# Small latent projections of branch D placed between the big projection blocks, in a two-layer trunk kernel

## What is computed

```
h = _rms(x, p['norm1_g']) * (1 + sc1) + sh1
aq, ak, av, bq, bk, bv, cq, ck, cv, dqa, dckv, dkr, gates = _split_in(h @ p['w_in'])
aq = pos(_rms(aq.reshape(B, T, A_HEADS, 2, A_QK), p['a_qk_g'][0]))
...
dq = (_rms(dqa, p['d_qnorm_g']) @ p['w_d_qb']).reshape(B, T, D_HEADS, D_QK)
dq = _rms(dq, p['d_qk_g'][0])
dckv = _rms(dckv, p['d_kvnorm_g'])
kd, vd = _mla_kv(dckv, dkr, p['w_d_kvb'], p['d_qk_g'][1])
```

## Time and profile before

| | us |
|---|---|
| median of 3 runs | 5418.61 (5416.52 to 5420.11) |
| profiled execution | 5413.07 |
| its span | 5411.3 |
| PE busy | 5099.5 (94%) |
| DVE busy | 3206.5 (59%) |
| ACT, POOL busy | 1676.5, 1325.4 |
| this stage, layer 0 and layer 1 | 241.1 and 234.6 |

### The profile page before, as it was taken

The page is one execution under the profiler, slowest core; times in us unless marked ns, Lnnn a source line. Parts: engine busy times, 40 slices in busy tenths (PEclk is TensorE's granted clock), DMA queues, the critical chain, the costliest instruction groups (busy, mean ns, idle before and its releaser), DMA issues.

```text
span 5411.3 us, 68396 instructions
## 1 busy us (share of the span) xinstructions
PE 5099.5 (94%) x25512; PEld 4124.9 (76%) x25512; DVE 3206.5 (59%) x7229; ACT 1676.5 (31%) x2610; POOL 1325.4 (24%) x858
## 2 busy tenths in 40 slices
PE   4979999889999999999989799998899999999999
PEld 1846688677888887888868467877788888788887
DVE  1556411107998995666654763111488998766666
ACT  2325422222333332222232353212233333322222
POOL 1310022214344331111123001213244344211111
PEclk6978999999999999999999799999999999999999
DMA  6200021264877878888831001222367877888886
GB/s 228 71 29 1 11 73 65 74 242 170 270 239 260 281 258 308 289 288 291 293 121 58 15 1 35 68 65 66 131 219 263 280 261 239 316 286 294 291 288 222
DMA packets 349128, 981.98 MB, mean 181 GB/s; under 512 B 31648, under 2 KB 100128, under 8 KB 345504
## 3 DMA queue, kind: packets, MB, share of 16 engines
q1 hardware_dynamic: 215232, 553.19, 31.6%
q0 software_dynamic: 74880, 276.86, 14.6%
q10 hardware_dynamic: 58720, 148.04, 7.0%
HBM read 829.43 MB, written 148.54 MB: 181 GB/s over the span
## 4 chain that ended last, share of the span: by engine, by line
PE 84%; DVE 6%; DMA 3%; ACT 3%; POOL 1%; issue 1%; DVEq 1%; ACTq 0%; POOLq 0%; SPq 0%
PE PS L813 26%; PE PS L773 23%; PE PS L474 15%; PE PS L463 5%; PE PS L795 4%; PE PS L601 3%; PE PS L627 2%; PE PS L464 1%; DVE AR L1183 1%; PE PS L611 1%; POOL HR L1516 1%; PE PS L571 1%; DMA WR<-in_ada 1%; PE PS L761 1%; DVE SM L1222 1%
## 5 line engine op out<-in xcount | busy, mean ns | idle before, releaser
L813 PE MATMUL PS<-HB,VR 128*128 128x512 f32 x6144 | 1397.1, 390 | 17.2 <-DVE HB L1473 17.2
L813 PEld LDWEIGHTS PS<-HB,VR 128*128 128x128 f32 x6144 | 1156.3, 188 | 258.0 <-issue 18.0
L773 PE MATMUL PS<-HR,UR 128*128 128x512 f32 x4128 | 1013.0, 399 | 0.0
L1516 POOL TENSOR_TENSOR UR<-WR,UR 128x1024 fp32r<-128x1024 f32 x212 | 530.6, 2504 | 1838.7 <-ACT UR L995 938.0
L474 PE MATMUL PS<-HR,UR 128*128 128x320 f32 (+1 forms) x5952 | 924.0, 315 | 44.0 <-POOL HR L1516 38.8
L474 PEld LDWEIGHTS PS<-HR,UR 128*128 128x128 f32 x5952 | 888.4, 190 | 69.9 <-issue 47.6
L773 PEld LDWEIGHTS PS<-HR,UR 128*128 128x128 f32 x4128 | 768.2, 190 | 166.9
L1460 DVE TENSOR_TENSOR VR<-HT,VR 128x1024 fp32r<-128x1024 f32 x256 | 313.8, 1226 | 459.7 <-ACT VR L1113 374.4
L1113 ACT CAST VR<-HT 128x1024 fp32r<-128x1024 f32 x256 | 268.8, 1050 | 962.7 <-PE PS L813 960.2
L773 PE MATMUL PS<-HR 128*128 128x512 f32 x2016 | 486.7, 394 | 0.0
L773 PEld LDWEIGHTS PS<-HR 128*128 128x128 f32 x2016 | 372.1, 188 | 73.6
(11 more groups left out here) (183 smaller groups left out, 5975.4 us busy)
## 6 DMA issues: line engine op xcount, KB each, us to landing
WR<-in_uT SPq DMA_DIRECT2D x256, 512.0 KB
HT<-in_vtab SPq DMA_DIRECT2D x256, 512.0 KB, 4.0
activations<-AR ACTq DMA_DIRECT2D x256, 256.0 KB
gates_by_expert<-AR ACTq DMA_DIRECT2D x128, 512.0 KB, 3.5
HW<-activations SPq DMA_DIRECT2D x256, 256.0 KB
WR<-gates_by_expert SPq DMA_DIRECT2D x64, 1024.0 KB
WR<-in_wgate SPq DMA_DIRECT2D x64, 640.0 KB, 3.9
WR<-in_ada SPq DMA_DIRECT2D x24, 1024.0 KB, 4.9
```

What stands on the lines that cost most here:

```text
L773: last = pe.matmul(bank(n % 2), u_part(n, w)[:, c, :], HR[:, h, c, 0:LAT], start=c == 0 and i == 0, stop=c == DC - 1 and i == 2)
L813: last = pe.matmul(bank(d), VR[:, m % 4, w, P * d:P * d + P], HB[:, (m + 1) % 3, h, :], start=m == 0 and i == 0, stop=m == E1 - 1 and i == 2)
L1516: nc.gpsimd.tensor_tensor(dst, src, high.bitcast(F32), ALU.subtract).then_inc(sem_, 1)
```

## The change

The items get a new order: qa, qa, ckv, kr, aq, aq, ak, and from there a small item after each big block: dq0, ak, dk0, bq, dq1, bq, dk1, bk, dq2, cq, dk2, cq, dq3, ck, dk3. `d_values` comes behind them, and `values` comes last, in another order of token tiles, with the last two rotations between its first three blocks. The small items' weights leave the ring: those of dq and of the values of D are loaded at once into the tail columns of all four slots (which only gate blocks used), those of dk into a free part of HT. STD moves from VD to VT, since VT is now written last. The semaphores are counted anew.

```diff
-    items = ([("aq", 0), ("aq", 1), ("ak", 0), ("ak", 1), ("bq", 0), ("bq", 1), ("bk", 0), ("cq", 0), ("cq", 1),
-              ("ck", 0), ("qa", 0), ("qa", 1), ("ckv", 0), ("kr", 0)]
-             + [("dq", h) for h in range(HEADS)] + [("dk", h) for h in range(HEADS)])
+    items = [("qa", 0), ("qa", 1), ("ckv", 0), ("kr", 0), ("aq", 0), ("aq", 1), ("ak", 0), ("dq", 0), ("ak", 1), ("dk", 0),
+             ("bq", 0), ("dq", 1), ("bq", 1), ("dk", 1), ("bk", 0), ("dq", 2), ("cq", 0), ("dk", 2), ("cq", 1), ("dq", 3),
+             ("ck", 0), ("dk", 3)]
...
-        STD = VD.rearrange("p a b -> p (a b)").rearrange("p (a b) -> p a b", a=2)
+        STD = VT[:, 0:3, :].rearrange("p a b -> p (a b)").rearrange("p (a b) -> p a b", a=2)
...
+                sp.dma_start(WR[:, :, D:SLOT], wdq[l]).then_inc(d_in, 16)
                 sp.wait_ge(hr_ready, l * (2 * DC) + DC)
...
+                sp.dma_start(WDK.rearrange("p h d -> p (h d)"), wkv[l]).then_inc(d_in, 16)
...
-                load(l, B_DQ, WR[:, B_DQ % RING, 0:2 * HEADS * D_QK], wdq[l])
-                load(l, B_KV, WR[:, B_KV % RING, 0:HEADS * (D_QK + HD)], wkv[l])
...
+            VALUE_TILES = (3, 2, 4, 1, 0)
+
+            def values(l, n):
+                if n == 0:
+                    pe.wait_ge(y_ready, (l + 1) * NI)
+                pe.wait_ge(split, l * N_SPLIT + (SPLIT_NO[B_V + n] + 1))
+                w = UR[:, SPLIT_NO[B_V + n] % 2]
+                for t in VALUE_TILES:
+                    if n == 0 and t == 4:
+                        pe.wait_ge(dv_out, l + 1)
...
-                for s in range(NI + 2):
-                    if s == N_FM:
-                        values(l)
+                for s in range(NI + 1):
                     if s < NI:
                         if items[s] == ("dk", 0):
                             pe.wait_ge(l_in, l * 96 + 80)
                             pe.wait_ge(yn_ready, l * NN + (norm_no[at_item["ckv", 0]] + 1))
                         project(l, s)
-                    if 1 <= s <= NI:
+                    else:
+                        d_values(l)
+                    if s >= 1:
                         head_sums(l, s - 1)
-                    if s >= 2:
+                    if 2 <= s < NI:
                         rotate(l, s - 2)
-                d_values(l)
+                values(l, 0)
+                rotate(l, NI - 2)
+                values(l, 1)
+                rotate(l, NI - 1)
+                for n in range(2, N_V):
+                    values(l, n)
                 phase_end(pe, l, 1)
...
-                for s in range(NI + 1):
-                    if s < N_FM:
-                        high(l, B_FM + s + 2)
-                    if s == N_FM:
-                        for n in range(2, N_V):
-                            high(l, B_V + n)
-                        used(l, B_V + N_V - 1)
-                        for t in range(TILES):
-                            nc.scalar.copy(VT[:, t if t < 4 else 5, :], bank(t if t < 4 else 7)).then_inc(v_out, 1)
-                    if s < NI:
-                        raw(l, s)
+                for s in range(NI):
+                    if s in block_of:
+                        high(l, B_FM + block_of[s] + 2)
+                    raw(l, s)
                     if s >= 1:
                         std(l, s - 1)
-                used(l, B_KV)
+                act.wait_ge(dv_ready, l + 1)
+                nc.scalar.copy(VD[:, 0:4, :].rearrange("p a b -> p (a b)"), PF[:, 0:1024])
+                nc.scalar.copy(VD[:, 4:6, :].rearrange("p a b -> p (a b)"), bank(7)).then_inc(dv_out, 1)
+                std(l, NI - 1)
+                for n in range(2, N_V):
+                    high(l, B_V + n)
+                used(l, B_V + N_V - 1)
                 act.wait_ge(yn_ready, (l + 1) * NN)
-                nc.scalar.copy(VD.rearrange("p a b -> p (a b)"), PF[:, 0:256 * KTILES])
+                for t in range(TILES):
+                    nc.scalar.copy(VT[:, t if t < 4 else 5, :], bank(t if t < 4 else 7))
```

More of the change, by code:

```diff
@@ L72, in loads @@
     first = N_ADA if l else 0
-    pairs = 0 if l else sum(m % RING == n % RING for m in range(N_ADA) if m < n)
-    before = loads(l - 1, BLOCKS + n % RING) if l else 0
-    return before + (n - first) // RING - (pairs if n % 2 else 0)
+    own = sum(m % RING == n % RING and m not in (B_DQ, B_KV) and (m >= N_ADA or m % 2 == 0) for m in range(first, n))
+    return own + (loads(l - 1, BLOCKS + n % RING) if l else 0)
 def block_no(l, n):
@@ L299, in build @@
         v_out = sem("v_out")
+        d_in, dv_ready, dv_out = sem("latent_weights_in"), sem("latent_values"), sem("latent_values_out")
         st_out = sem("states_out")
@@ L513, in project @@
                 if kind == "dq":
[L514 removed]
                     if j == 0:
+                        pe.wait_ge(d_in, 32 * (l + 1))
                         pe.wait_ge(yn_ready, l * NN + (norm_no[at_item["qa", 1]] + 1))
[L517 removed]
                     for kc in range(2):
[L519 to L521 removed]
+                        last = both(cols(base, D_QK), WDQ[:, j, kc, :], lambda lo, hi: QA[:, kc, lo:hi], kc == 0, kc == 1)
+                    last.then_inc(pj_ready, 1)
                 elif kind == "dk":
[L523 to L524 removed]
+                    both(cols(base, D_QK), WDK[:, j, :], lambda lo, hi: KT[:, 4, lo:hi], True, False, KEYS)
                     both(cols(base, D_QK), sel_kr, lambda lo, hi: KR[0:D_ROPE, lo:hi], False, True, KEYS).then_inc(pj_ready, 1)
                 else:
[L527 removed]
+                    part = halves(l, B_FM + block_of[n])
                     for c in range(DC):
@@ new lines, in values @@
+            def values(l, n):
[6 more added lines that the diff above has]
+                        pe.wait_ge(dv_out, l + 1)
+                    for cc in range(2):
+                        c = 2 * n + cc
+                        for m, (h, x) in enumerate(((0, 0), (1, 0), (0, 1))):
+                            last = pe.matmul(bank(t if t < 4 else 7), HR[:, h, c, qcols(t)], w[:, x, cc * 512:(cc + 1) * 512],
+                                             start=c == 0 and m == 0, stop=c == DC - 1 and m == 2)
+                last.then_inc(w_used, 1 if n < N_V - 1 else B_GATE - B_DQ + 1)
@@ L575, in d_values @@
             def d_values(l):
-                pe.wait_ge(y_ready, l * NI + NI)
-                w = weights(l, B_KV)
+                pe.wait_ge(y_ready, l * NI + NI - 1)
                 for t in range(KTILES):
-                    last = pe.matmul(PF[:, 256 * t:256 * t + 256], KT[:, 4, qcols(t)], w[:, HEADS * D_QK:HEADS * (D_QK + HD)],
-                                     start=True, stop=True)
-                last.then_inc(w_used, 1)
+                    at = 256 * t if t < 4 else 3584 + 256 * (t - 4)
+                    last = pe.matmul(PF[:, at:at + 256], KT[:, 4, qcols(t)], WDV, start=True, stop=True)
@@ L583, in scores @@
+                last.then_inc(dv_ready, 1)
             def scores(l, u):
@@ L862, in raw @@
                 base = 1024 * (n % 2)
[L864 to L865 removed]
+                if n in block_of:
+                    used(l, B_FM + block_of[n])
                 else:
[L867 removed]
+                    act.wait_ge(pj_ready, l * (2 * HEADS) + small_no[n] + 1)
                 if kind == "kr":
```

32 lines of the change are left out of this document (17 added, 15 removed).

## The result

The changed kernel took 5440.94 us (median of 7 runs, 5434.6 to 5455.9) where the kernel before took 5418.61 beside it (7 runs, 5410.5 to 5422.0): ratio 1.0046, 95% interval 1.0035 to 1.0057. That is 22.3 us slower. Its profiled execution took 5439.9 (span 5438.1), against 5413.07 before.

A forecast was written before the change was run, and what follows sets the result against it. PE bounds the big blocks, DVE and ACT's chain the small items; mixed, a serial ring binds. Layer 1 9.0 plus layer 0 2.5 makes 11.5 us slower: 5430.1 from the 5418.61 median, range 5408 to 5446.

The forecast's parts named there:

- ring of PE, ACT and DVE: Mixed big and small items: std, norm, rope, rotation, next big block run without overlap; seven per layer, 20.25 or 21.3 us.
- Front: Layer 1's projections up to the seventh big block: it ends at 2863.2 instead of 2871.3, 8.1 us gained.
- old first rotation: First rotation in the kernel before: a slow norm write under POOL's cast, then a lowered clock; 3.8 us saved.
- The ring without the clock: Time per pair of big and small item at full clock: 18.35 us with dq or aq, 19.4 with dk.
- The clock's price: PE restarts at a lowered clock after 5.2 to 5.4 us idle per pair: 1.9 us lost, bounds 1.7 and 2.25.
- Tail: Layer 1 from dq3's rotation through d_values and values to the last copies: 3018.4 to 3057.9, nothing in values waiting.
- Layer 0: Its new projection stage takes the same 243.6 us as layer 1's, against 241.1 before: 2.5 us slower.
- The clock that stays up: Rival: PE's clock stays up between small items' rotations and big blocks; sixteen restarts at 1.9 us go, 5400; chance 0.08.
- No ring: Rival: the wait closes nothing, DVE bounds each pair at 15.3 or 16.3 us; about 5360; chance 0.04.
- A cheaper ring: Rival: the ring stands but costs a little less, such as restarts of 1.7 us; 5421 to 5429; chance 0.36.
- Long low stretches: Rival: two or three rings a layer at half speed for all PE work, 15 to 20 us more; 5448; chance 0.06.
- DMA issues, POOL's casts and the wait for dv_out: Projection stage: said to cost nothing, being covered by other work; 3 to 4 us a layer if the DMA cover failed.

The follow-up runs named there:

- e1: The changed kernel with each rotation one step later on PE, behind the next big block: 5380.24 us, ratio 0.9936.
- e2: The changed kernel with 4 or 6 useless products in PE's idle time ahead of each small item's rotation: 5400.44 us, ratio 0.9966.
- e5: The kernel before with only its big blocks reordered to begin with qa, qa, ckv, kr: 5413.27 us, ratio 1.0005.
- e10: Second run of the changed kernel with rotations one step later and the small item's std ahead of the big block's copy: 5354.03 us, ratio 0.9888.
- e0: The changed kernel once more, unedited: 5442.27 us, ratio 1.0043.
- e3: The changed kernel with the small item's std ahead of the big block's copy and square on ACT: 5458.51 us, ratio 1.0074.

## Why the prediction was right, and where it wasn't

**Direction, place and mechanism held, the size less.** The forecast was 5430 and slower, the result 5440.94 and slower, within 5408 to 5446. But the sum said 11.5 us slower and 22.3 were measured, nearly twice as much. The whole loss was to be in this stage, in a ring of PE, ACT and DVE, and e1 (the ring opened, 36 us a layer gained) and e2 (its idle time filled, 18 gained) show both halves of that.

**Front: right.** 48.9 us from the chain's start to the seventh block's end: forecast 2863.2 less 2814.3, measured 2821.26 to 2870.20 (2862.91 plus 7.29). The norm and POOL's cast no longer met. Of the 8.1 us, 3.8 were put on the old first rotation; e5 gave 2.9 in layer 1.

**The ring without the clock: right.** The seven spacings sum to 148.84 us (2880.55 to 3029.39). Rotation start to block end took 11.02, 10.59, 9.91, 10.01, 11.14, 10.70 and 9.98 us (each from its two rows), 73.35 in all, where seven warm ones are 56.0. With the 17.35 of difference taken off, 131.5 us are left for seven rings, against 4 times 18.35 and 3 times 19.4, which is 131.6.

**The clock's price: the term that was too small.** The prediction took 1.9 us for a restart, with 1.7 and 2.25 as bounds, behind 5.2 to 5.4 us of idle time. The idle time was 4.4 us ahead of a dq's rotation and 6.0 ahead of a dk's. Measured: 17.35 over seven, 2.5 each, from 1.9 to 3.1 (against the 8.12 that e2 showed for a warm pair, 2.4 each). So this mean is above the upper bound. Seven times 0.6 is 4 us a layer, and layer 1's stage missed the forecast by 3.8 (247.4 against 243.6). In layer 0 the same seven cost 17.04, so this term makes up nearly 8 of the 10.8 us that the sum lacked. In the second profile of the changed kernel the mean was 2.2 and 2.3, about the upper bound. The upper bound was drawn from a single place, some 4.5 us of low clock from 3015.20 on, and the start behind 8.43 us of idle time, low for 4.2 us, lies below it; here it lasted some 6 us after 5.19. A bound from one or two restarts is no bound. That the error went towards slower is luck: with a wake of about 1.2 us the prediction's own sum changes its sign. The Trainium skill's page "TensorE: Matmul & The Clock Gate", section "Loop structure matters more than you think", names as cold a loop with a wait of 8 us in every round; the trace agrees in kind with waits of 4.4 to 6.0, and only in part, since the ring began at 0.50 but its block ran on at 1.00 from 2887.

**Tail: right.** Rotation of dq3 to the end of the copies: forecast 39.5 (3018.4 to 3057.9), measured 39.3 (3029.39 to 3068.65). Nothing in it waited but the barrier.

**Layer 0: right for the new stage, unlucky in the old.** The forecast gave both layers the same time, and they have it (247.2 and 247.4). But it compared with a layer 0 that was long in that one profile: 260.9 by the barriers, against 255.9 and 252.7 in two more. By the means of three profiles of before and two of after, the stage costs 266.1 less 256.5 in layer 0 and 266.6 less 254.2 in layer 1, 22.0 us in all, which is nearly all of the 22.3 measured. A stage time from one execution was the second weak point.

**Rivals.** The clock that stays up: excluded by the row of 2880 to 2886.7 at 0.50. No ring: excluded in the change as written, and just what e10 shows once the rotation moves. A cheaper ring: the opposite held. Long low stretches through two or three whole rings: not seen, but the restarts were long enough to cost about half of what that rival asked. DMA issues, POOL's casts and the wait for dv_out cost PE nothing, as said: behind the first row its only waits in the stage were the eight for rope and the barrier's.

**Not forecast: attention.** Nothing was said of stages that aren't touched. In the two profiles compared it gave 6.6 us more (9.0 in layer 1, 2.4 less in layer 0). How much of the 22.3 it makes up can't be said from two profiles whose attention stages span 260 to 281 us; the stages and the medians agree without it.

## What to carry to other kernels

An in-order engine that waits for one small dependent product holds back all the dense work queued behind it. When a slow chain on one engine is mixed with dense work on another, place the dependent product behind the next dense block, not ahead, if its buffers allow it: here the same instructions went from 0.4% slower to 0.6% faster by one step's shift, and to about 1% with std moved too. Price each wait twice, as idle time and as clock afterwards, take the latter from several restarts, and a stage's time from several executions.

## What was not expected of the hardware

- A restart of PE after 4.4 to 6.0 us of idle time cost 1.9 to 3.1 us, and the idle time's length didn't order them: 3.1 after one of 6.00, 1.9 after another of 6.00, 2.6 after 4.38. Layer 0 has the same seven in the same order to 0.15 us, but in layer 1 of e0, with the same waits, they are 1.5, 1.7, 3.0, 2.6, 1.9, 2.0 and 3.2. In layer 1 of e3 three restarts after 3.3 us cost 2.8 to 3.0, three after 5.11 about 2.5. What sets the price of a single restart stays open.
- Attention, unchanged, lay at a few distinct times in layer 1 of the fourteen profiles: 257.4 (three), 263.7 to 267.6 (eight), 275.0 (three), with the granted clock at 0.92, 0.87 to 0.89 and 0.83, whatever stood directly ahead.
- In e10 a norm's product over 512 columns took 2.70 us where others take 0.75 (another took 2.96), POOL's low part beside it, as in the earlier trace rows. The two rows, DVE and POOL:

```profile
2858.01 2.70 DVE L1200 SCALAR_TENSOR_TENSOR AR<-AR,GN 128x512 f32<-128x512 f32 x1
...
2857.82 2.35 POOL L1528 TENSOR_TENSOR UR<-WR,UR 128x1024 fp32r<-128x1024 f32 x1 [4.97 <-ACT UR L958]
```

The Trainium skill's page "SBUF — State Buffer" says that VectorE and GpSimd share a pair of ports, that where a VectorE instruction has two inputs in SBUF and GpSimd's reads SBUF the first to start holds it for its whole length, and that the other is fully blocked meanwhile. The rows agree: POOL's subtraction began 0.19 us earlier, and the product ended 0.54 us after POOL's subtraction did (2860.71 against 2860.17), close to its own time alone. With DVE as the bound of the faster version, this meeting is now on its path.
